# The out projection's last four columns by token tile, and a later place for tile 1's half

## The chip, the cores and the metric

The kernel runs on one core of a Trainium2 chip. The metric is the device time of one execution in microseconds (us). Three runs of the kernel before took 1156.49, 1156.77 and 1157.5 us; the median is 1156.77 us. The engines are TensorE (PE; its weight loads are PEld), VectorE (DVE), ScalarE (ACT), GpSimd (POOL) and SyncE (SP, which only issues DMAs).

## The reference, cut to what matters

There are 256 tokens of width 1024, everything is float32. A first block is run once, then two layers of a second block. Of the first block, this is what the change touches:

```
x = x + gate1 * (y_mix @ w_out)                              # out projection, 1024 x 1024
h2 = rms_norm(x, norm2_w) * (1.0 + scale2) + shift2
q = (h2 @ peer_wq).reshape(..., 8 heads, 2, 128)             # queries of eight expert heads
s = einsum('bqhpd,hpnd->bqhpn', q, peer_subkeys)             # scores of 2 x 128 keys
vals, idx = top_k(s, 16); combo = all 256 sums; top_s, pos = top_k(combo, 16)
u_sel = peer_u[expert]; a = gelu(einsum('bqhkd,bqd->bqhk', u_sel, h2))
x = x + gate2 * einsum('bqhk,bqhkd->bqd', softmax(top_s) * a, peer_v[expert])
```

`gate1`, `scale2`, `shift2` and `gate2` come from a modulation, `silu(c) @ w_ada + b_ada`. Each of 256 tokens picks 16 of 16384 experts for each of 8 heads, and for each pick a row of `peer_u` and one of `peer_v` is fetched: 2048 floats, 8 KB.

## The kernel before, in words

The 256 tokens are two tiles of 128. Activations lie feature by token: `xT[:, c, :]` holds features 128c to 128c+127 of all tokens, c = 0 to 7. Each engine runs its own program in the order in which it is written, and engines wait for one another's counters (semaphores), so that the order in which lines stand in an engine's program sets the order of the work.

**Out projection.** Each weight piece (128 output columns) is split by ScalarE and VectorE into two rounded parts (`split_hi`, L699, and `split_lo`, L706), and the activations too. A product is then three TensorE matmuls for each of eight 128-feature chunks (`by_parts`, L1447 to L1449): 24 matmuls of 256 tokens for a column of 128 features. Columns 0 to 3 are written to two PSUM banks (`held_out`), and columns 4 to 7 follow by `whole(mixed_in, 2)`, twice. After each column VectorE adds it to `xT` (L2210, the last one by tile, L2221), and ScalarE squares the sum (L1184) and multiplies it by the norm's gain (`gain_x`, L1174, for tile 0; L1179 for tile 1). TensorE adds the squares over features with a matrix of ones (`out_sums`, L1674); it does so in three places between the columns.

**First head.** Head 0's query for tile 0 is computed before the norm's root is known: `query_products` (L1689) on `xg`, then `early_scores_of_head_0` (L1767, L1768); the root's reciprocal is multiplied on the scores afterwards (`scores_of_head_0`, L2015). `route_first` then picks the first 8 of head 0's 16 experts for tile 0, `route_rest` the others. The normed `hT` of both tiles (`second_norm`, L2001) is shifted (L1211), turned to token-major (`turn_h2`, L1702), and used for the other queries (`score_query`, L1717) and keys (L1730).

**Gathers.** There are 16 groups (2 tiles x 8 heads) of 16 picks. Pick n is one indirect DMA of GpSimd (L997) of 128 rows of 8 KB, 1 MB, into one of 14 places. The places are six pairs in `rows`, seven in `low_pairs` (where the rounded parts and the squares of the projection lie before) and one slot of the weight ring; `FIRST_ROUND` gives their order. GpSimd waits before a place's first use until what lay there has been used, and later until `pair_used` says that TensorE has added the pick before. VectorE multiplies a gathered row by the token (`dot`, L2293), ScalarE sums it (L1260), takes gelu (L1271) and scales a diagonal (L1276), and TensorE adds the weighted second half of the row to the sum in PSUM (L1742). VectorE also chooses the experts of group g + 2 while group g is worked on (`route_halves`, `route_pairs`, `route_experts`); the second group's choice, `route(1)`, stands behind the first group's dots 0 to 3 and two more (`DOTS_AHEAD = 2`).

**Other work around it.** The modulation's 48 tiles are multiplied and summed on VectorE (`ada_dots`, L1965; the last two, `last_ada_tile`, L1975), those for `scale2` to `gate2` between the columns of the out projection. SP loads the expert heads' weights, and at the end of the out projection (`proj` at `M1`) the first weight unit of the second block's layers into `low_pairs[:, 1, :]` (L873). Where TensorE waits for ScalarE's copy of head 0's scores, it runs eight matmuls whose result nobody reads (L1803).

```
            whole(mixed_in, 2)
            out_sums(0, 1, 2, 3)
            whole(mixed_in, 2)
            out_sums(4, 5)
```

Of the kernel before, what the change touches and what calls it, by code (L numbers as in the profile page):

```python
# [14 lines left out]
ALU = mybir.AluOpType  # L15
# [32 lines left out]
PLACES = [("rows", 0), ("rows", 1), ("low", 2), ("low", 3), ("low", 4), ("low", 5), ("rows", 2), ("rows", 3), ("rows", 4), ("rows", 5),  # L48
          ("low", 0), ("low", 6), ("ring", 0), ("low", 7)]
LAST_ROUND = tuple(range(10))  # L50
# [3 lines left out]
AHEAD = 2  # L54
DOTS_AHEAD = 2
EXPERTS = 4
# [249 lines left out]
def first_of(*place):  # L306

    return PLACE_OF.index(PLACES.index(place))
# [55 lines left out]
def build(nc, a, out):  # L364
    ctx = ExitStack()
    with ctx:
# [53 lines left out]
        class Area:  # L420
# [66 lines left out]
        FIRST_HEADS_AT = ADA_RING * D  # L487
        own_place = {OWN_UNIT: own_unit, HELD_QUERY: low_pairs[:, 7, :], LAST_QUERY: extra[:, 0:2 * D], N1: low_pairs[:, 1, :]} | {n: extra[:, 2 * D + 512 * i:2 * D + 512 * i + 512] for i, n in enumerate(SUB_UNITS)} | \
            {n: flat[:, FIRST_HEADS_AT + 2 * D * i:FIRST_HEADS_AT + 2 * D * i + AT_1[n + 1] - AT_1[n]] for i, n in enumerate(FIRST_HEADS)}
# [137 lines left out]
        def chunk_out(m, width=T):  # L627
            b, j, _, _ = SEATS_1[m]
            z = aux[:, 3 + b, :] if b < BATCH else pj[:, b % 2, :]
            return z[:, j * T:j * T + width]  # L630

        conv_sums = chunk_out(M1 - KC + 2)

        def chunk_wait(eng, m):
# [149 lines left out]
        def tile_of(t):  # L784
            return slice(t * P, (t + 1) * P)
# [39 lines left out]
        def _(sp):  # L825
# [21 lines left out]
            for n in LOAD_ORDER:  # L847
# [75 lines left out]
        def _(pool):  # L923
# [45 lines left out]
            for g in range(NT * EXPERT_HEADS):  # L969
# [6 lines left out]
                for j in range(PICKS):  # L976
# [41 lines left out]
        def _(act):  # L1018
# [162 lines left out]

            for c in range(KC - 1):
# [4 lines left out]
                if c < KC - 2:  # L1187
                    gain_x(c)
                if c in (1, 3):
                    round_to(31 if c == 1 else 32)  # L1190
                if c in (3, 4, 5):
                    gain_x_of_tile_1(2 * c - 6, 2 * c - 5)
            act.wait_ge(taken_dve, KC)
            nc.scalar.activation(sq[:, KC - 1, 0:P], xT[:, KC - 1, 0:P], ACT.Square).then_inc(squares, 1)
            gain_x(KC - 2)
            gain_x(KC - 1)
            act.wait_ge(taken_dve, KC + 1)
            nc.scalar.activation(sq[:, KC - 1, P:T], xT[:, KC - 1, P:T], ACT.Square).then_inc(squares, 1)
            gain_x_of_tile_1(KC - 2, KC - 1).then_inc(xg_ready, 1)

# [230 lines left out]
        def _(pe):  # L1431
# [236 lines left out]

            def out_sums(*columns, tiles=range(NT)):

                for k in columns:
                    for t in tiles:
                        pe.wait_ge(squares, k + 1 if k < KC - 1 else KC + t)
                        ins = mm(aux[:, 2 + t, 0:P], ones[:, :], sq[:, k, t * P:(t + 1) * P], start=(k == 0), stop=(k == KC - 1))  # L1674
                        if k == KC - 1:
                            ins.then_inc(sums, 1)
# [127 lines left out]
            pe.wait_ge(taken_dve, KC + 1)  # L1804
            pe.wait_ge(h_ready, 2 * KC)
# [149 lines left out]
        def _(dve):  # L1955
# [247 lines left out]

            for c in range(KC):
                if c in (2, 4):
                    low_to(28 + c)
                m = M1 - KC + c
                chunk_wait(dve, m)
                if c < KC - 1:
                    v.scalar_tensor_tensor(xT[:, c, :], chunk_out(m), mod[:, 2 * KC + c:2 * KC + c + 1], xT[:, c, :], ALU.mult, ALU.add) \  # L2210
                        .then_inc(taken_dve, 1)
                    if c in (2, 3):
                        ada_dots(38 + c, 39 + c)
                    elif c in (4, 5):
                        ada_dots(34 + 2 * c, 36 + 2 * c)
                    if c == 5:
                        last_ada_tile(0)
                else:
                    for t in range(NT):
                        ts = slice(t * P, (t + 1) * P)  # L2220
                        v.scalar_tensor_tensor(xT[:, c, ts], chunk_out(m)[:, ts], mod[:, 2 * KC + c:2 * KC + c + 1], xT[:, c, ts], ALU.mult, ALU.add) \  # L2221
                            .then_inc(taken_dve, 1)
            last_ada_tile(1)
            last_ada_bias()
            dve.wait_ge(taken_dve, KC + 1)
            rstd_by_token()
            second_rstd(0)
            second_norm(0)
            scores_of_head_0()
# [144 lines left out]

            route_first()
            second_rstd(1)
# [331 lines left out]
```

## Time and profile before

| | |
|---|---|
| median of 3 runs | 1156.77 us |
| profiled execution, its own time | 1157.3 us |
| span of that execution's instructions | 1155.3 us |
| PE busy | 1040.5 us (90%) |
| DVE busy | 855.9 us (74%) |
| ACT busy | 708.2 us (61%) |
| POOL busy | 344.8 us (30%) |
| gathers (software queue q0) | 268.45 MB |
| weights and inputs (queue q1) | 120.10 MB |

The shares of busy time are means over stages with different limits: until about 165 us the first block's projections and attention, then the gathers, then the two layers of the second block. In the page's strip of 40 slices (28.9 us each) the DMA engines move 421 GB/s in nearly every slice from the 8th to the 28th.

### The profile page before, as it was taken

The numbers are of one execution on the slowest core, as the hardware profiler recorded it, in microseconds if no ns is written. First come the engines' busy times: TensorE is split into PE (matmuls) and PEld (weight loads), VectorE is DVE, ScalarE is ACT, GpSimd is POOL, SyncE is SP. The second block draws the span as 40 slices with busy tenths as digits, with TensorE's granted clock in tenths as the row PEclk, the third lists the DMA queues.
The fourth block names the chain that finished last, engine by engine and source line by source line (L and its number), as shares of the span: only waits on it lengthen the run. The fifth ranks groups of instructions, "written<-read, shape, count | busy, mean of one in ns | idle before, by whom it ended". The sixth has DMA issues, their size and how long they took to land.

```text
span 1155.3 us, 13406 instructions
## 1 busy us (share of the span) xinstructions
PE 1040.5 (90%) x4687; PEld 724.8 (63%) x4687; DVE 855.9 (74%) x1525; ACT 708.2 (61%) x1410; POOL 344.8 (30%) x367
## 2 busy tenths in 40 slices
PE   8999998999999878778877877799999999999997
PEld 6999987554455333333333323299888888888885
DVE  6998987967677666766767776656677768886776
ACT  3635855777766776666677666761458554577451
POOL 1001014555544554545544544555000000400000
PEclk9999999999999999999988999999999999999999
DMA  9988869999999999999999999999954654455540
GB/s 371 407 332 305 342 233 410 421 421 421 421 421 422 421 421 421 421 418 420 422 398 423 422 421 421 422 415 420 358 217 163 238 186 178 178 187 186 206 155 37
DMA packets 59556, 390.00 MB, mean 338 GB/s; under 512 B 6881, under 2 KB 7905, under 8 KB 15714
## 3 DMA queue, kind: packets, MB, share of 16 engines
q0 software_dynamic: 36864, 268.45, 56.1%
q1 hardware_dynamic: 21152, 120.10, 27.7%
q8 instruction: 37, 0.61, 0.2%
q10 hardware_dynamic: 1474, 0.60, 0.2%
q14 instruction: 29, 0.24, 0.1%
HBM read 388.08 MB, written 1.05 MB: 337 GB/s over the span
## 4 chain that ended last, share of the span: by engine, by line
PE 53%; DMA 27%; ACT 7%; issue 6%; DVE 5%; POOL 1%; SPq 0%; ACTq 0%; POOLq 0%; DVEq 0%
PE aux L1742 15%; DMA rows<-in_peer_uv,work 12%; DMA low_pairs<-in_peer_uv,work 12%; PE pj L1795 6%; PE pj L1796 6%; PE pj L1797 6%; PE pj L1855 5%; PE aux L1717 3%; PE pj L1856 3%; PE aux L1748 3%; ACT low_pairs L1260 2%; DMA wring<-in_peer_uv,work 2%; ACT L1271 1%; PE pj L1447 1%; DMA rows<-in_w_ada 1%
## 5 line engine op out<-in xcount | busy, mean ns | idle before, releaser
L1742 PE MATMUL aux<-rows,work 128*128 128x512 f32 x480 | 230.0, 630 | 49.9 <-ACT work L1276 49.9
L1742 PE MATMUL aux<-low_pairs,work 128*128 128x512 f32 x384 | 184.3, 629 | 37.5 <-ACT work L1276 37.5
L1742 PEld LDWEIGHTS aux<-rows,work 128*128 128x128 f32 x480 | 94.5, 201 | 176.5 <-issue 109.2
L997 POOL DMA_INDIRECT rows<-in_peer_uv,work x140 | 135.5, 968 | 227.3 <-PE aux L1742 146.9
L1260 ACT ACTIVATE rows<-rows 128x1024 f32<-128x1024 f32 x128 | 134.6, 1052 | 80.0 <-DVE rows L2293 79.7
L1742 PEld LDWEIGHTS aux<-low_pairs,work 128*128 128x128 f32 x384 | 75.6, 201 | 138.8 <-issue 87.2
L1260 ACT ACTIVATE low_pairs<-low_pairs 128x1024 f32<-128x1024 f32 x104 | 109.3, 1051 | 62.5 <-DVE low_pairs L2293 62.4
L775 DVE TENSOR_TENSOR wlo<-wring,whi 128x1024 fp32r<-128x1024 f32 x98 | 121.1, 1251 | 32.5 <-ACT whi L769 31.7
L997 POOL DMA_INDIRECT low_pairs<-in_peer_uv,work x108 | 103.5, 958 | 125.3 <-PE aux L1742 107.2
L769 ACT CAST whi<-wring 128x1024 fp32r<-128x1024 f32 x98 | 101.4, 1050 | 51.3 <-PE pj L1856 26.6
L2293 DVE TENSOR_TENSOR rows<-rows,aux 128x1024 f32<-128x1024 f32 x66 | 80.0, 1219 | 53.2 <-DMA rows<-in_peer_uv,work 52.8
L2293 DVE TENSOR_TENSOR low_pairs<-low_pairs,pj 128x1024 f32<-128x1024 f32 x58 | 70.1, 1218 | 45.1 <-DMA low_pairs<-in_peer_uv,work 44.3
L2293 DVE TENSOR_TENSOR rows<-rows,pj 128x1024 f32<-128x1024 f32 x62 | 74.7, 1217 | 38.5 <-DMA rows<-in_peer_uv,work 38.3
L1855 PE MATMUL pj<-x_parts,whi 128*128 128x512 f32 x256 | 91.3, 400 | 0.1
L1276 ACT ACTIVATE work<-work 128x128 f32<-128x128 f32 x248 | 79.3, 390 | 8.9 <-POOL work L966 3.1
L2293 DVE TENSOR_TENSOR low_pairs<-low_pairs,aux 128x1024 f32<-128x1024 f32 x46 | 55.8, 1219 | 35.8 <-DMA low_pairs<-in_peer_uv,work 35.3
L1447 PE MATMUL pj<-x_parts,whi 128*128 128x256 f32 x256 | 73.5, 287 | 0.4 <-DVE wlo L706 0.2
L1795 PE MATMUL pj<-whi,x_parts 128*128 128x512 f32 x184 | 72.6, 395 | 0.0
L1448 PE MATMUL pj<-x_parts,whi 128*128 128x256 f32 x256 | 72.5, 283 | 0.0
L1449 PE MATMUL pj<-x_parts,wlo 128*128 128x256 f32 x256 | 72.5, 283 | 0.0
L1856 PE MATMUL pj<-x_parts,wlo 128*128 128x256 f32 x256 | 72.0, 281 | 0.0
L1797 PE MATMUL pj<-wlo,x_parts 128*128 128x512 f32 x184 | 71.8, 390 | 0.0
(351 smaller groups left out, 2067.6 us busy)
## 6 DMA issues: line engine op xcount, KB each, us to landing
wring<-in_w SPq DMA_DIRECT2D x74, 1024.0 KB, 4.9
rows<-in_w_ada SPq DMA_DIRECT2D x46, 512.0 KB, 9.4
rows<-in_w SPq DMA_DIRECT2D x3, 1024.0 KB, 11.5
rows<-in_peer_uv,work POOLq DMA_INDIRECT x140, 12.8
low_pairs<-in_w SPq DMA_DIRECT2D x2, 1024.0 KB, 7.5
work<-in_late_rows SPq DMA_DIRECT2D x2, 1024.0 KB, 9.2
xT<-in_gate_rows SPq DMA_DIRECT2D x2, 1024.0 KB, 6.8
rows<-in_norm_rows SPq DMA_DIRECT2D x2, 1024.0 KB, 7.2
```

The source lines that it names most:

```text
L769: nc.scalar.copy(layer_part("hi", l, p), layer_raw(l, p)).then_inc(w_hi, 1)
L775: dve.tensor_tensor(layer_part("lo", l, p), layer_raw(l, p), full(layer_part("hi", l, p)), ALU.subtract).then_inc(w_lo["d"], 1)
L997: pool.indirect_dma_start(out=pair(n), out_offset=None, in_=a["peer_uv"], in_offset=bass.IndirectOffsetOnAxis(ap=expert[g % EXPERTS][:, j: ...
L1260: nc.scalar.activation(pair(n)[:, 0:D], pair(n)[:, 0:D], ACT.Copy, accum_out=dots[g % 2][:, j:j + 1]).then_inc(dotted, 1)
L1276: nc.scalar.activation(diag[:, j, :], diag[:, j, :], ACT.Copy, scale=act_dots[g % 2][:, j:j + 1]).then_inc(diag_ready, 1)
L1447: mm(o, w[0], x[0], start=start, stop=False, skip_group_check=skip)
L1742: ins = mm(peer_sum[t][:, half(c)], diag[:, n % PICKS, :], pair(n)[:, D + c * 512:D + (c + 1) * 512], start=(n % (EXPERT_HEADS * PICKS) == ...
L1795: mm(bank(u), hi[:, k, ts], w_hi_[:, j, :], start=(k == 0), stop=False)
L1797: ins = mm(bank(u), hi[:, k, ts], w_lo_[:, j, :], start=False, stop=(k == last))
L1855: mm(both, w_hi_[:, k, :], x_parts[:, :, k, :], start=(k == 0), stop=False, skip_group_check=True)
L1856: ins = mm(bank(u)[:, 0:T], w_lo_[:, k, :], xh[:, k, :], start=False, stop=(k == KC - 1), skip_group_check=True)
L2293: v.tensor_tensor(row, row, h2_tok[g // EXPERT_HEADS], ALU.mult).then_inc(multiplied, 1)
```

## The change

Columns 4 to 7 of the out projection are no longer multiplied for all 256 tokens at once. `tile_products(0)` multiplies the four columns for tile 0's 128 tokens, and `tile_products(1)`, for tile 1, stands behind `early_scores_of_head_0`. Sums of squares are made once for each tile behind its columns (`out_sums(t)`). VectorE adds columns 0 to 3 whole, columns 4 to 7 of tile 0 next, and those of tile 1 behind `route_first`. The modulation's dots move: 42 to 44 behind tile 0's columns, 45 and the last two behind `route_rest`. ScalarE's squares and gains follow the new order. `DOTS_AHEAD` goes from 2 to 0, so that `route(1)` stands ahead of dot 4. The idle matmuls go from eight to four. The layers' first weight unit goes to `low_pairs[:, 0, :]` and waits for tile 1's second column; the gathers use `low_pairs[:, 1, :]` instead. GpSimd gets three new waits.

```
-          ("low", 0), ("low", 6), ("ring", 0), ("low", 7)]
+          ("low", 1), ("low", 6), ("ring", 0), ("low", 7)]
-DOTS_AHEAD = 2
+DOTS_AHEAD = 0
+KEEP_BUSY = 4
...
+        TILES_FROM = M1 - HC
+        def tile_out(c, t):
+            if c < KC - 1:
+                return chunk_out(TILES_FROM, 512)[:, (c - HC) * P:(c - HC + 1) * P]
+            return chunk_out(M1 - 2)[:, t * P:(t + 1) * P]
+        def tile_wait(eng, c, t):
+            eng.wait_ge(proj, TILES_FROM + t * HC + (HC - 1 if c < KC - 1 else HC))
+        def taken_of(c, t):
+            return c + 1 + (t * HC if c >= HC else 0)
...
-            sp.wait_ge(proj, M1)
+            sp.wait_ge(proj, M1 + 2)
             sp.dma_start(own_place[N1], a["w2"][0, 0]).then_inc(own_loaded[own_group(N1)], 16)
...
+                    if n == first_of("rows", 1):
+                        pool.wait_ge(ada_used, RING_TILES - 1)
+                    if n == first_of("low", 2):
+                        pool.wait_ge(proj, M1 + HC)
+                    if n == first_of("low", 6):
+                        pool.wait_ge(sums, 1 + NT)
...
+            def square_tile(c, t):
+                act.wait_ge(taken_dve, taken_of(c, t))
+                nc.scalar.activation(sq[:, c, halves_[t]], xT[:, c, halves_[t]], ACT.Square).then_inc(squares, 1)
...
-            root(0)
             for s in range(2):
                 act.wait_ge(early_products, s + 1)
                 nc.scalar.copy(pq[:, 0, s, 0:P + 1], aux[:, 4 + s, 0:P + 1]).then_inc(early_query_out, 1)
+            root(0)
             act.wait_ge(early_products, 3)
             nc.scalar.copy(s_all[:, 0, :], aux[:, 1, 0:2 * KEYS]).then_inc(early_query_out, 1)
+            for c in range(HC, KC - 1):
+                square_tile(c, 1)
+            gain_x_of_tile_1(*range(HC, KC - 1))
+            square_tile(KC - 1, 1)
+            gain_x_of_tile_1(KC - 1).then_inc(xg_ready, 1)
             root(1)
...
-            whole(mixed_in, 2)
-            out_sums(0, 1, 2, 3)
-            whole(mixed_in, 2)
-            out_sums(4, 5)
+            def tile_products(t):
+                ts = tile_of(t)
+                for c in range(HC, KC):
+                    n = first_tiled + c - HC
+                    split_wait(pe, n)
+                    hi, lo = parts(n)
...
+                    for k in range(KC):
+                        xh_, xl_ = mixed_in(k)
+                        ins = by_parts(tile_out(c, t), (hi[:, k, :], lo[:, k, :]), (xh_[:, ts], xl_[:, ts]), k == 0, k == KC - 1, skip=True)
+                    ins.then_inc(proj, 1)
+            def out_sums(t):
+                for k in range(KC):
+                    pe.wait_ge(squares, taken_of(k, t))
+                    ins = mm(aux[:, 2 + t, 0:P], ones[:, :], sq[:, k, t * P:(t + 1) * P], start=(k == 0), stop=(k == KC - 1))
+                ins.then_inc(sums, 1)
+            tile_products(0)
...
             for s in range(2):
-                query_products(s, range(HC))
-            out_sums(6, 7, tiles=(0, ))
+                query_products(s, range(KC - 1))
             for s in range(2):
-                query_products(s, range(HC, KC)).then_inc(early_products, 1)
-            out_sums(6, 7, tiles=(1, ))
+                query_products(s, (KC - 1, )).then_inc(early_products, 1)
+            out_sums(0)
...
             early_scores_of_head_0()
+            tile_products(1)
+            out_sums(1)
             pe.wait_ge(early_query_out, 3)
-            for _ in range(8):
+            for _ in range(KEEP_BUSY):
...
+            for c in range(HC):                                  # VectorE: columns 0 to 3 whole
...
+                if c == 1:
+                    low_to(30)
+            low_to(32)
+            ada_dots(40, 42)
+            for c in range(HC, KC):
+                add_tile(c, 0)
+            ada_dots(42, 45)
             rstd_by_token()
-            second_rstd(0)
-            second_norm(0)
             scores_of_head_0()
...
             route_first()
+            for c in range(HC, KC - 1):
+                add_tile(c, 1)
+            second_rstd(0)
+            add_tile(KC - 1, 1)
+            second_norm(0)
             second_rstd(1)
             second_norm(1)
             route_rest()
+            ada_dots(45, RING_TILES)
+            for n in range(LAST_TILES):
+                last_ada_tile(n)
+            last_ada_bias()
```

## Rows read from the trace of the kernel before

**Rows 1.** The page, part 3: queue, kind, packets, MB, share of 16 engines.
```profile
q0 software_dynamic: 36864, 268.45, 56.1%
```

**Rows 2.** Stretches: us, engines' busy time (instructions), PEclk, DMA share, GB/s.
```profile
165.00:170.00 5.00, 4.76 (x26) 3.90 (x25) 4.62 (x20) 2.96 (x10) 0.51 (x1) 1.00 0.00 0
220.00:400.00 180.00, 167.87 (x478) 88.11 (x477) 124.85 (x231) 128.89 (x278) 93.99 (x99) 0.98 1.01 421
...
600.00:800.00 200.00, 162.24 (x621) 94.30 (x620) 129.34 (x210) 125.25 (x267) 103.40 (x109) 0.93 1.01 419
```

**Rows 3.** Timeline of TensorE: start, us, engine, line, operation, out<-in, count.
```profile
145.49 0.28 PE L1447 MATMUL pj<-x_parts,whi 128*128 128x256 f32 x1
...
151.25 1.95 PE L1674 MATMUL aux<-low_pairs,ones 128*128 128x128 f32 x16
...
158.79 1.05 PE L1674 MATMUL aux<-low_pairs,ones 128*128 128x128 f32 x8
159.68 1.95 PE L1689 MATMUL aux<-work,rows 128*128 128x129 f32 x16
...
164.82 0.39 PE L1768 MATMUL aux<-rows,pq 128*128 128x128 f32 x2
```

**Rows 4.** Timeline of TensorE, narrow f32 products of the attention.
```profile
124.19 1.90 PE L1604 MATMUL aux<-work,rows 128*128 128x64 f32 x16
125.92 1.95 PE L1638 MATMUL pj<-low_pairs,ones 128*128 128x256 f32 x8
```

**Rows 5.** Timeline of TensorE's weight loads behind a stall.
```profile
134.10 0.19 PEld L1447 LDWEIGHTS pj<-x_parts,whi 128*128 128x128 f32 x1 [0.34 <-DVE x_parts L2175]
134.20 0.19 PEld L1448 LDWEIGHTS pj<-x_parts,whi 128*128 128x128 f32 x1
```

**Rows 6.** Timeline of GpSimd, issues of gathers 0, 1, 2, 12 and 21.
```profile
169.49 1.18 POOL L997 DMA_INDIRECT rows<-in_peer_uv,work  x1 [53.56 <-DVE work L2333]
170.97 1.21 POOL L997 DMA_INDIRECT rows<-in_peer_uv,work  x1 [0.30 <-issue]
172.48 0.93 POOL L997 DMA_INDIRECT low_pairs<-in_peer_uv,work  x1 [0.30 <-issue]
...
197.09 0.98 POOL L997 DMA_INDIRECT wring<-in_peer_uv,work  x1
...
220.09 0.94 POOL L997 DMA_INDIRECT rows<-in_peer_uv,work  x1 [3.73 <-PE aux L1742]
```

**Rows 7.** DMA issues, last number us to landing: gathers 0, 1, 12, 21.
```profile
rows<-in_peer_uv,work POOLq DMA_INDIRECT x1, 5.8
rows<-in_peer_uv,work POOLq DMA_INDIRECT x1, 9.0
wring<-in_peer_uv,work POOLq DMA_INDIRECT x1, 10.2
rows<-in_peer_uv,work POOLq DMA_INDIRECT x1, 9.6
```

**Rows 8.** Timeline of SP's queue: the layers' first weight unit.
```profile
158.98 0.33 SPq L873 DMA_DIRECT2D low_pairs<-in_w  x1
```

**Rows 9.** Timeline of VectorE and ScalarE: tile, root, reciprocal, multiply, dots 0 and 3.
```profile
160.62 1.22 DVE L1975 CUSTOM_DVE_ANT_0 work<-work,rows 128x1024 f32<-128x1024 f32 x1
162.12 0.36 ACT L1204 ACTIVATE rstd<-aux,eps 128x128 f32<-128x128 f32 x1
163.07 0.94 DVE L1995 RECIPROCAL rstd<-rstd 128x128 f32<-128x128 f32 x1
170.14 1.23 DVE L2001 TENSOR_TENSOR hT<-hT,rstd 128x1024 f32<-128x1024 f32 x1
176.55 1.22 DVE L2293 TENSOR_TENSOR rows<-rows,pj 128x1024 f32<-128x1024 f32 x1
184.97 1.22 DVE L2293 TENSOR_TENSOR low_pairs<-low_pairs,pj 128x1024 f32<-128x1024 f32 x1 [1.27 <-DMA low_pairs<-in_peer_uv,work]
```

**Rows 10.** The chain that ended last, in order of time, 140 to 210 us.
```profile
188.91 6.91 PE aux L1717 x32
```

More of the change, by code:

```diff
@@ L487, in build @@
         FIRST_HEADS_AT = ADA_RING * D
-        own_place = {OWN_UNIT: own_unit, HELD_QUERY: low_pairs[:, 7, :], LAST_QUERY: extra[:, 0:2 * D], N1: low_pairs[:, 1, :]} | {n: extra[:, 2 * D + 512 * i:2 * D + 512 * i + 512] for i, n in enumerate(SUB_UNITS)} | \
+        own_place = {OWN_UNIT: own_unit, HELD_QUERY: low_pairs[:, 7, :], LAST_QUERY: extra[:, 0:2 * D], N1: low_pairs[:, 0, :]} | {n: extra[:, 2 * D + 512 * i:2 * D + 512 * i + 512] for i, n in enumerate(SUB_UNITS)} | \
             {n: flat[:, FIRST_HEADS_AT + 2 * D * i:FIRST_HEADS_AT + 2 * D * i + AT_1[n + 1] - AT_1[n]] for i, n in enumerate(FIRST_HEADS)}
@@ L1180, in gain_x_of_tile_1 @@
                 return ins
-            for c in range(KC - 1):
+            def square_tile(c, t):
+                act.wait_ge(taken_dve, taken_of(c, t))
+                nc.scalar.activation(sq[:, c, halves_[t]], xT[:, c, halves_[t]], ACT.Square).then_inc(squares, 1)
+            round_to(30)
+            for c in range(HC):
                 act.wait_ge(taken_dve, c + 1)
@@ L1186, in _ @@
                     nc.scalar.copy(xg[:, :, P:P + 1], mod[:, 3 * KC:4 * KC].unsqueeze(2)).then_inc(xg_ready, 1)
[L1187 to L1195, printed above, removed]
+                gain_x(c)
+                if c < 2:
+                    round_to(31 + c)
+            gain_x_of_tile_1(*range(HC))
+            for c in range(HC, KC - 1):
+                act.wait_ge(taken_dve, taken_of(c, 0))
+                gain_x(c)
+            square_tile(HC, 0)
+            act.wait_ge(taken_dve, taken_of(KC - 1, 0))
             gain_x(KC - 1)
-            act.wait_ge(taken_dve, KC + 1)
-            nc.scalar.activation(sq[:, KC - 1, P:T], xT[:, KC - 1, P:T], ACT.Square).then_inc(squares, 1)
-            gain_x_of_tile_1(KC - 2, KC - 1).then_inc(xg_ready, 1)
+            for c in range(HC + 1, KC):
+                square_tile(c, 0)
             def root(t):
@@ L1667, in _ @@
                 ins.then_inc(proj, 1)
[L1669 to L1676, printed above, removed]
-            whole(mixed_in, 2)
-            out_sums(0, 1, 2, 3)
-            whole(mixed_in, 2)
-            out_sums(4, 5)
+            def tile_products(t):
[4 more added lines that the diff above has]
+                    hi, lo = parts(n)
+                    if t:
+                        pe.wait_ge(taken_dve, taken_of(KC - 2 if c < KC - 1 else KC - 1, 0))
+                    else:
+                        pe.wait_ge(taken_dve, 2 if c < KC - 1 else HC)
+                    for k in range(KC):
[7 more added lines that the diff above has]
+                ins.then_inc(sums, 1)
+            first_tiled = piece[0]
+            tile_products(0)
             query_of_head_0 = w_slot(FIRST_HEADS[0])
@@ L1800, in _ @@
             early_scores_of_head_0()
+            tile_products(1)
+            out_sums(1)
             pe.wait_ge(early_query_out, 3)
-            for _ in range(8):
+            for _ in range(KEEP_BUSY):
                 mm(aux[:, 1, 0:2 * P], ident[:, :], wsT[:, 0:2, :].rearrange("p g t -> p (g t)"), start=True, stop=True)
-            pe.wait_ge(taken_dve, KC + 1)
+            pe.wait_ge(taken_dve, KC + HC)
             pe.wait_ge(h_ready, 2 * KC)
@@ L2202, in _, with add_tile @@
             second_gain()
-            for c in range(KC):
-                if c in (2, 4):
-                    low_to(28 + c)
+            def add_tile(c, t):
+                ts = slice(t * P, (t + 1) * P)
+                tile_wait(dve, c, t)
+                v.scalar_tensor_tensor(xT[:, c, ts], tile_out(c, t), mod[:, 2 * KC + c:2 * KC + c + 1], xT[:, c, ts], ALU.mult, ALU.add) \
+                    .then_inc(taken_dve, 1)
+            for c in range(HC):
                 m = M1 - KC + c
                 chunk_wait(dve, m)
[L2209 to L2225, printed above, removed]
+                v.scalar_tensor_tensor(xT[:, c, :], chunk_out(m), mod[:, 2 * KC + c:2 * KC + c + 1], xT[:, c, :], ALU.mult, ALU.add) \
+                    .then_inc(taken_dve, 1)
+                if c == 1:
[5 more added lines that the diff above has]
+            ada_dots(42, 45)
             rstd_by_token()
-            second_rstd(0)
-            second_norm(0)
             scores_of_head_0()
@@ L2375, in _ @@
             route_first()
+            for c in range(HC, KC - 1):
+                add_tile(c, 1)
+            second_rstd(0)
+            add_tile(KC - 1, 1)
+            second_norm(0)
             second_rstd(1)
```

## The prediction

> **What bounds the kernel now.** I read the queues and the stretches first. The gathers of the expert rows are 268.45 MB, and from 220 us to 800 us the DMA engines are busy all the time at 419 to 421 GB/s [rows 1, 2], while no compute engine is full. One gather is 1.05 MB and so takes 2.49 us. So the middle of the program is a queue of 256 gathers, and two things set its end: when it starts, and whether it ever runs dry. Between 165 and 170 us nothing moves at all [rows 2]: this hole in front of the first gather is what an edit can shorten.
>
> Then the timelines of TensorE, VectorE and GpSimd around the hole. TensorE multiplies the out projection's last four columns from 145.49 to 158.79 (96 products of 256 columns, and 16 sums of squares between them), then makes head 0's query and keys until 165.04 [rows 3], VectorE chooses eight experts, and GpSimd issues the first gather at 169.49 [rows 6].
>
> Last, how far the queue is ahead of its consumers. The first gather, alone in the queue, landed 5.8 us after its issue. The 13th (index 12, issue 197.09) took 10.2 us and the 22nd (index 21, issue 220.09) 9.6 us [rows 6, 7], so they lay 4.4 and 3.8 us behind others. Those are the margins: an issue that comes later by more than that leaves the queue empty. Up to the 13th gather the chain of waits runs not through the queue but from the first group's dots over ScalarE to head 2's query on TensorE [rows 9, 10].
>
> **The change, step by step.** All sums are against the profiled execution, 1157.3 us, 0.5 us above the median of the runs (1156.77); I add the difference to the median.
>
> (1) Tile 0's half of the last four columns: 4 x 8 x 3 = 96 products of 128 moving columns instead of 256. Before shows no such product of rounded parts. A 256-column one starts every 0.12 us (48 from 145.49 to 151.25) [rows 3]. If only the columns counted, a 128-column one would take 0.06. But the products in plain f32 don't get cheaper with fewer columns: 16 records of 64 columns took 1.73 us, 0.108 each, and 8 of 128 columns 0.89, 0.111 each [rows 4, 3]; each loads its own weights. After a stall the second weight load of the rounded parts starts 0.10 us after the first [rows 5], long before a matmul's columns could hold it up. So I take 0.108, the weight load's pace: 10.4 us for tile 0, done at 155.9. Ends: 0.06 (columns alone) and 0.21 (two f32 records for each product, were narrow products run like plain f32).
>
> The Trainium skill ("TensorE: Matmul & The Clock Gate", section "Back-to-back issue gap") gives about 81 ns for a matmul of 128 columns in a stream of load and matmul. By it tile 0 would be done at 153.3. The 0.108 of the narrow f32 rows speaks against it; no row here shows it for rounded parts.
>
> (2) From there to the first gather: before 6.25 us (158.79 to 165.04: sums, query, scores). After: the query's 3.6, tile 0's 16 sum records in 1.7, scores 0.9, together 6.2. The choice of eight experts is unchanged. First gather: 2.9 + 0.1 = 3.0 us earlier, at 166.5.
>
> (3) The layers' first weight unit (1 MB, SP) was issued at 158.98 into the empty queue [rows 8]. It now waits for tile 1's second column: 162.0 + 48 x 0.108 = 167.2, behind the first gather. It takes 2.49 us of a queue that is full from there: the lead shrinks to 0.5 us.
>
> (4) Tile 1's 96 products and 16 sums now stand behind the first head's keys: 162.0 + 10.4 = 172.4. VectorE idles from the end of the first choice (166) until tile 1's three columns are there (170). Then come the last column's add, square and sum (0.3 us each, estimated from the root's 0.36), root, reciprocal (0.94) and the multiply for tile 1 (1.1) [rows 9]: done at 176.9, where before the multiply began at 170.14 and the choice's rest ended at 176.55. The rest takes 5.3 us, to 182.2.
>
> (5) Three dots of the modulation (1.15 each) and the bias, before beside the projection, now stand between that and the first dot: 3.8 us, 186.0. The first four dots (4.7 us) end at 190.8. Before, they waited for data, and the fourth began at 184.97: it comes 4.7 us later.
>
> (6) From the fourth dot the chain is as before: ScalarE's sum, head 1's keys, head 2's query (6.9 us on TensorE [rows 10]), its keys, the first weighted sums, whose ends free the places for the 14th gather on. So the 13th and 14th gathers issue 4.7 us later, the later ones some 5.0, as dots 5 and 6 now stand behind the second group's choice and that behind head 2's scores; score_query(3) on TensorE hides nearly all of it.
>
> (7) Sum at the queue: index 12 is late by 4.7 - 4.4 = 0.3 us, index 21 by 5.0 - 3.8 = 1.2. The largest counts: +1.2. The lead of (3) lies before it and is lost. Starting from nearly empty costs more: behind the first gather the second landed not 2.49 but 4.7 us later (issue 170.97 plus 9.0 against 169.49 plus 5.8 [rows 6, 7]), a loss of 2.2. Here it is between nothing and that; I take 1.1. Together **+2.3 us: 1159.1**.
>
> At nothing: the third gather waits for tile 1's products (172.6, before 172.48 [rows 6]) with the first two and the weight unit in the queue until 176. The ninth waits for the last modulation dots (185.9), which has cover: it lands seven gathers behind the second, which landed at 180.0, so at 197.4, and an issue at 191.6 would still do. Half of the keep-busy products go, at a place where TensorE waits anyway. The low places that change sides, the earlier splits of the last two pieces and ScalarE's new order have idle time around them. If (5)'s dots had other cover, 3.8 us would come back, more than the margin lacks.
>
> **Rivals.**
> A. Columns set the pace, wholly (0.06 us) or half way to the weight load (0.084). For it: no narrow product of rounded parts is in the trace. Against: the f32 rows. The first gather comes 7.6 to 5.2 us earlier; the weight unit, issued 1.4 us before it or right with it, takes 0.7 to 2.5 of that; the consumers are 4.5 us early to 0.4 late, within the margins. 1149.9 to 1154.1, say 1152. The skill's 81 ns would be a case of A, 1153.7; of A's chance I give it a third.
> B. Narrow products cost two f32 records, 0.21 us. For it: f32 128 x 128 is recorded so; against: the rounded 256-column rows show no second record. Tile 1 ends 20 us later, so index 21 is late by 25 - 3.8, and with the restart: 1179.
> C. Not slower: the pace is as in (1), but the consumers' delay stays under the margin. It decides at the fourth dot: if it comes less than 3.5 us later (begins before 188.5), the queue never empties and the start alone counts: 0.5 us, or up to 2.5 if the weight unit only fills the 2.2 us that the start loses anyway. 1154.3 to 1156.3, say 1155.5. For it: VectorE has 4 us idle at 166 to 170, and each hop of (4) is estimated; against: (4) and (5) are in strict order on VectorE.
>
> **How the numbers follow.** Forecast 49%; its own range, from pace 0.106 and no restart loss to 0.12 and the whole loss, is +0.8 to +5.7: 1157.6 to 1162.5. A 18%, B 10%, C 23%. A measurement of this kernel tells 0.2%, 2.3 us, from no change; the forecast sits on that bound: of its 49, 25 slower, 22 same, 2 faster. A: 16 faster, 2 same. B: slower. C: 12 faster, 11 same. Faster 30%, same 35%, slower 35%. The range holds the forecast, C and about half of A: 1151.0 to 1163.5; B and A's far end stay outside.
>
> **What would show it.** Right: narrow products start every 0.11 us; the first gather near 166.5; the weight unit's load between the first two gathers; the fourth dot near 189.6; between 195 and 230 us stretches of the DMA under 400 GB/s. Wrong in (1): starts every 0.06 to 0.08 us, first gather before 164. Wrong in (4) or (5): fourth dot before 188.5 and the DMA at 420 GB/s throughout; then the end moves by the start alone. B: starts every 0.2 us, first gather after 175.

## The result and the profile after

The changed kernel is slower: 1162.8 us (median of 6 runs, 1161.25 to 1164.03) against 1157.11 us for the kernel before beside it (6 runs), a ratio of 1.0049, 95% interval 1.0037 to 1.0061, so 4.3 to 7.1 us. The two profiled executions lie 4.0 us apart (1161.25 and 1157.3; spans 1159.3 and 1155.3).

The start went as forecast. TensorE's timeline of the changed kernel: the narrow products start every 0.11 us (145.83, 145.94, 146.05), and tile 0 is done at 156.22, where the query begins.
```profile
145.83 0.27 PE L1479 MATMUL pj<-x_parts,whi 128*128 128x128 f32 x1
145.94 0.27 PE L1480 MATMUL pj<-x_parts,whi 128*128 128x128 f32 x1
146.05 0.28 PE L1481 MATMUL pj<-x_parts,wlo 128*128 128x128 f32 x1
...
156.22 3.79 PE L1733 MATMUL aux<-work,rows 128*128 128x129 f32 x32
```
GpSimd's issues of gathers 0, 12 and 21 (index from 0), and SP's load of the layers' first weight unit, again the changed kernel. Against [rows 6, 8] the first gather is 2.5 us earlier, index 12 is 5.4 us later, index 21 6.6 us later, and the unit now stands behind the first gather and ahead of the second.
```profile
166.97 1.18 POOL L1019 DMA_INDIRECT rows<-in_peer_uv,work  x1 [51.00 <-DVE work L2373]
...
202.50 1.26 POOL L1019 DMA_INDIRECT wring<-in_peer_uv,work  x1
...
226.66 0.94 POOL L1019 DMA_INDIRECT rows<-in_peer_uv,work  x1 [3.73 <-PE aux L1785]
```
```profile
168.03 0.33 SPq L889 DMA_DIRECT2D low_pairs<-in_w  x1
```
What that did to the queue is read from three stretches (columns as in [rows 2]; the last number is GB/s). The kernel before:
```profile
165.00:180.00 15.00, 12.40 (x69) 11.20 (x69) 12.03 (x47) 8.09 (x25) 8.07 (x9) 0.89 0.55 199
180.00:200.00 20.00, 17.27 (x81) 13.74 (x80) 14.66 (x42) 11.25 (x24) 7.73 (x9) 1.00 1.01 424
200.00:230.00 30.00, 30.00 (x94) 16.74 (x93) 27.65 (x61) 23.42 (x49) 16.24 (x18) 1.00 1.01 421
```
The changed kernel, the same stretches:
```profile
165.00:180.00 15.00, 13.85 (x117) 13.32 (x117) 8.96 (x29) 7.07 (x25) 7.22 (x7) 1.00 0.74 294
180.00:200.00 20.00, 17.12 (x97) 15.11 (x96) 16.06 (x49) 11.45 (x26) 6.15 (x7) 1.00 1.02 424
200.00:230.00 30.00, 28.59 (x91) 16.29 (x90) 29.49 (x57) 21.39 (x45) 13.91 (x14) 1.00 0.90 339
```
TensorE's granted clock is 1.00 in all three rows of the changed kernel, so the clock is not what lost the time here. The rows make a ledger. Stretch times GB/s gives the bytes moved; from them I take the weight unit (1.05 MB) where it is loaded inside, and divide what is missing against before by 421 GB/s. By 200 us the changed kernel has moved 12.89 MB, 11.84 of them gathers, against 11.47: 0.9 us ahead. Between 200 and 230 us it moves 10.17 MB instead of 12.63: 5.8 us lost. By 230 us it is 2.09 MB, 5.0 us, behind. From there to 580 us both go at 421 GB/s, so this is most of the difference. In five-microsecond pieces all six from 200 to 230 us lie below 421, this one lowest (the others 328 to 413):
```profile
200.00:205.00 5.00, 4.49 (x20) 2.85 (x19) 4.83 (x18) 2.45 (x4) 2.45 (x3) 1.00 0.55 184
```
The gather of index 12 landed 5.8 us after its issue (the view of DMA issues), as long as the first one alone in the queue took in [rows 7]: the queue was dry when it came.
```profile
wring<-in_peer_uv,work POOLq DMA_INDIRECT x1, 5.8
```
Who was late is in VectorE's timeline of the changed kernel: idle until tile 1's columns (170.71), the three modulation dots from 183.08, the first dots at 186.90, the fourth half way through the next pair, at 190.4, and then 3.39 us of waiting for ScalarE's copy of head 1's scores before the second group's choice.
```profile
170.71 0.87 DVE L2253 SCALAR_TENSOR_TENSOR xT<-pj,mod,xT 128x128 f32<-128x128 f32 x3 [4.04 <-PE pj L1481]
...
183.08 1.22 DVE L2010 CUSTOM_DVE_ANT_0 rows<-rows 128x1024 f32<-128x1024 f32 x1
...
186.90 2.35 DVE L2333 TENSOR_TENSOR rows<-rows,pj 128x1024 f32<-128x1024 f32 x2
...
189.24 2.33 DVE L2333 TENSOR_TENSOR low_pairs<-low_pairs,pj 128x1024 f32<-128x1024 f32 x2
194.97 0.49 DVE L2282 MAX8 work<-work 128x8 f32<-128x128 f32 x2 [3.39 <-ACT work L1253]
```
There is one later difference. Near 600 us the kernel before falls below the full rate itself (the two rows below), and the changed kernel less (422 and 389 GB/s in the same two pieces). By 780 us the ledger has gone from 5.0 to 3.9 us.
```profile
596.00:600.00 4.00, 4.00 (x11) 1.83 (x10) 3.81 (x10) 2.09 (x6) 2.64 (x4) 1.00 0.94 340
600.00:604.00 4.00, 4.00 (x10) 1.71 (x9) 2.99 (x5) 3.68 (x7) 2.25 (x3) 1.00 1.01 352
```

### The profile page after: what moved, and what is told of

Read it like the earlier page. It is cut to its first block, busy times and chain, and to the rows that moved or that the text cites. A ratio compares the mean times of both kernels' runs of the same rounds, so it can differ in the third digit from the quotient of the medians.

```text
span 1159.3 us, 13594 instructions
## 1 busy us (share of the span) xinstructions
PE 1050.4 (91%) x4775; PEld 730.4 (63%) x4775; DVE 857.6 (74%) x1528; ACT 708.7 (61%) x1413; POOL 344.2 (30%) x367
## 3 DMA queue, kind: packets, MB, share of 16 engines
HBM read 388.08 MB, written 1.05 MB: 336 GB/s over the span
## 4 chain that ended last, share of the span: by engine, by line
PE 53%; DMA 27%; ACT 10%; DVE 8%; issue 2%; SPq 1%; POOL 0%; ACTq 0%; DVEq 0%; POOLq 0%
PE aux L1785 15%; DMA rows<-in_peer_uv,work 12%; DMA low_pairs<-in_peer_uv,work 10%; PE pj L1838 6%; PE pj L1839 5%; PE pj L1840 5%; PE pj L1900 5%; PE pj L1901 3%; DMA rows<-in_w_ada 3%; PE pj L1479 2%; ACT low_pairs L1292 2%; PE pj L1480 2%; PE pj L1481 2%; PE aux L1760 2%; DMA wring<-in_peer_uv,work 2%
## 5 line engine op out<-in xcount | busy, mean ns | idle before, releaser
L1785 PE MATMUL aux<-rows,work 128*128 128x512 f32 x480 | 232.4, 635 | 42.8 <-ACT work L1308 42.8
L1785 PE MATMUL aux<-low_pairs,work 128*128 128x512 f32 x384 | 188.3, 641 | 38.4 <-ACT work L1308 38.4
L1479 PE MATMUL pj<-x_parts,whi 128*128 128x256 f32 (+1 forms) x288 | 81.9, 284 | 0.4 <-DVE wlo L722 0.3
L1480 PE MATMUL pj<-x_parts,whi 128*128 128x256 f32 (+1 forms) x288 | 80.9, 281 | 0.0
L1481 PE MATMUL pj<-x_parts,wlo 128*128 128x256 f32 (+1 forms) x288 | 80.9, 281 | 0.0
L1901 PE MATMUL pj<-x_parts,wlo 128*128 128x256 f32 x256 | 71.8, 281 | 0.0
```

Of the source, the lines that this page charges most:

```text
L1479: mm(o, w[0], x[0], start=start, stop=False, skip_group_check=skip)
L1480: mm(o, w[0], x[1], start=False, stop=False, skip_group_check=skip)
L1481: return mm(o, w[1], x[0], start=False, stop=stop, skip_group_check=skip)
L1785: ins = mm(peer_sum[t][:, half(c)], diag[:, n % PICKS, :], pair(n)[:, D + c * 512:D + (c + 1) * 512], start=(n % (EXPERT_HEADS * PICKS) == ...
L1901: ins = mm(bank(u)[:, 0:T], w_lo_[:, k, :], xh[:, k, :], start=False, stop=(k == KC - 1), skip_group_check=True)
```

## The experiments

Theory E: the queue is dry at gathers 12 to 21 because VectorE's dots come late, and the end follows that. Rivals: the weight unit in front of the gathers is the cost (U); in the runs of moved dots, the first gathers' pace is what counts (G). All times stand beside runs of the kernel before on the same chip (1156.9 to 1157.3 us).

**1. e1_two_dots_ahead.** The fifth and sixth dot back ahead of the second group's choice.
```diff
-DOTS_AHEAD = 0
+DOTS_AHEAD = 2
```

> The changed kernel with DOTS_AHEAD back to 2. Theory, an empty queue: in the changed kernel the second group's choice waits 3.4 us for head 1's scores (start 194.97) while dots 4 and 5 stand behind it. With the two dots ahead they fill that wait; dot 7 ends 2.3 us earlier, the fifth weighted sum on TensorE begins 0.9 us earlier (it then waits for head 3's first query half), and the gathers from the 18th on come 0.9 us earlier. Gathers 12 and 13 are untouched. Time 0.9 us under the changed kernel's (about 1161.9). Rival, the weight unit or the extra TensorE work is the cost: no difference. Rival, the order of dots is the main cost: 3 us or more under it.

1161.33 us, ratio 1.0032 (1.0020 to 1.0045), which overlaps the changed kernel's interval. The trace shows what the number alone doesn't: the dots did close the distance between index 12 and 21, from 24.16 us to 23.00, as in [rows 6], but index 12 itself was 1.65 us later. TensorE's granted clock was 0.57 in the mean from 193 to 197 us, so mostly at the lower of its two levels (1.2 GHz), just as it took up head 1's keys after 2.44 us of idling; the changed kernel idles there as long and has 1.00. So this profiled execution is 0.08 us off the changed kernel's, and the run decides little. Five of its six runs took 1161.28 to 1161.42 us and one 1159.16; whether that one kept the higher clock, no trace shows. Gathers 12 and 21, and the stretch:
```profile
204.15 0.99 POOL L1019 DMA_INDIRECT wring<-in_peer_uv,work  x1
...
227.15 0.95 POOL L1019 DMA_INDIRECT rows<-in_peer_uv,work  x1 [3.72 <-PE aux L1785]
```
```profile
193.00:197.00 4.00, 3.68 (x14) 3.39 (x15) 1.95 (x8) 1.75 (x3) 0.95 (x1) 0.57 1.01 420
```

**2. e2_mod_dots_in_idle.** The last three modulation dots and the bias go into VectorE's idle time before tile 1.
```diff
             route_first()
+            ada_dots(45, RING_TILES)
+            for n in range(LAST_TILES):
+                last_ada_tile(n)
+            last_ada_bias()
...
             route_rest()
-            ada_dots(45, RING_TILES)
-            for n in range(LAST_TILES):
-                last_ada_tile(n)
-            last_ada_bias()
```

> The changed kernel with the last three modulation dots and their bias moved into VectorE's idle time behind the first choice (166.6 to 170.7 us). Theory, an empty queue: the first dot starts 3.8 us earlier (183.1), but head 1's query on TensorE then ends last (190.8), so head 1's keys and all behind come 2.0 us earlier: gather 12 at 200.5, which leaves the queue just not empty; a hole of about 1.3 us stays at gathers 17 and 18. Time 3 to 4.4 us under the changed kernel's: 1158.4 to 1159.8. Rival, the weight unit in the queue or TensorE's extra 10 us: no difference (1162.8).

1158.98 us, 1.0017 (1.0008 to 1.0026): by the medians 3.8 us come back. That the moved work takes as much on VectorE (183.08 to 186.90 above) is in part chance. The dots begin 3.5 us earlier (183.42), but head 1's query on TensorE now ends last (191.1), so that the second group's choice, index 12 (200.96) and index 21 (225.11) come only 1.5 us earlier, and the ledger gains 1.6.
```profile
193.43 0.49 DVE L2282 MAX8 work<-work 128x8 f32<-128x128 f32 x2 [5.34 <-ACT work L1253]
```
From 200 to 230 us the queue moves 367 GB/s in place of 339: E holds. Unexpected: the first two gathers took longer to issue (last section).

**3. e3_both_moves.** Both edits.

> Both edits of the two runs before together. Theory, an empty queue: gathers 12 and 13 2.0 us earlier, 17 and 18 2.9 us earlier than in the changed kernel; almost no hole is left and the start's lead of 0.9 us counts: 1156.2 to 1157.5, no slower than before the change. Rivals: weight unit or TensorE's work, 1162.8; dots' order alone, as with DOTS_AHEAD 2 alone.

1157.61 us, 1.0007 (0.9997 to 1.0016): no longer told from before, 0.1 us above the range expected. By the medians the two moves together give back 5.2 of 5.7 us, with the weight unit and TensorE's extra work still in: those are not what cost the time. Beside e2 the two dots are worth 1.4 us: the choice begins when it did there (193.36, in e2 193.43), and from index 12 (200.88) to 21 (223.88) it is 23.00 us again. In e1 the wait ahead of the choice had room for the dots too (2.05 us of it were left); there the lower clock took the gain.

**4. e4_two_loads.** The narrow products cheaper: the weights' high part is loaded once for 256 moving columns (both parts of the tile's input), the low part for 128; VectorE adds the two halves.
```diff
-  ins = by_parts(tile_out(c, t), (hi[:, k, :], lo[:, k, :]), (xh_[:, ts], xl_[:, ts]), k == 0, k == KC - 1, skip=True)
+  mm(tile_out(c, t), hi[:, k, :], x_parts[:, :, k, ts], start=(k == 0), stop=False, skip_group_check=True)
+  ins = mm(tile_out(c, t)[:, 0, :], lo[:, k, :], xh_[:, ts], start=False, stop=(k == KC - 1), skip_group_check=True)
```

> The changed kernel with the tile products made from two weight loads a chunk instead of three: the high weights once, over 256 moving columns (the tile's high and low activations side by side), and the low weights once over 128; VectorE adds the two halves with one more operation each. Theory, the weight load sets the pace (0.111 us for a narrow product): a column takes 8 x (0.12 + 0.111) = 1.85 us instead of 2.67, a tile 7.4 instead of 10.7; the first gather comes 3 us earlier (164.0), tile 1 ends 6.6 us earlier, no hole is left in the queue, and the start counts: 3 to 4 us under the kernel before (1153 to 1154). Rival, the columns set the pace (0.06 us for 128): a column would take 8 x 0.18 = 1.44. Rival, one third fewer instructions saves nothing because the adds on VectorE are what the chain waits for: first gather 1 us or less earlier.

1157.13 us, 1.0000 (0.9991 to 1.0009): a miss. The products do start every 0.23 us for two, where three took 0.33, and the first gather goes out at 164.01, 5.5 us before [rows 6]. But index 12 is issued at 197.31 and the consumers are no earlier than in before: TensorE takes up head 1's keys at 188.00, in before at 187.78.
```profile
145.81 0.34 PE L1712 MATMUL pj<-x_parts,whi 128*128 128x256 f32 x1
145.99 0.23 PE L1713 MATMUL pj<-x_parts,wlo 128*128 128x128 f32 x1
146.05 0.33 PE L1712 MATMUL pj<-x_parts,whi 128*128 128x256 f32 x1
```
```profile
164.01 1.18 POOL L1017 DMA_INDIRECT rows<-in_peer_uv,work  x1 [47.97 <-DVE work L2380]
...
197.31 1.26 POOL L1017 DMA_INDIRECT wring<-in_peer_uv,work  x1
```
The stretches of this run show the lead made and lost: 389 GB/s in place of 199 up to 180, then 392 and 381 in place of 424 and 421. Its ledger at 230 us is 0.1 us behind before.
```profile
165.00:180.00 15.00, 12.81 (x93) 11.59 (x93) 12.06 (x35) 9.40 (x30) 8.29 (x8) 1.00 0.99 389
180.00:200.00 20.00, 17.06 (x80) 13.59 (x79) 16.12 (x53) 11.22 (x23) 7.86 (x9) 1.00 0.97 392
200.00:230.00 30.00, 29.11 (x90) 16.20 (x89) 27.52 (x55) 22.32 (x48) 15.45 (x17) 1.00 0.98 381
```
The slack of [rows 7] is not a constant: a queue that starts x us earlier and goes at the same rate meets each late gather x us sooner. A lead and a margin are the same microseconds.

**5. e5_unit_later.** The changed kernel, the weight unit loaded where the queue is full.
```diff
             sp.wait_ge(proj, M1 + 2)
+            sp.wait_ge(queries, 10)
```

> The changed kernel with one more wait: the layers' first weight unit (1 MB) is loaded only after head 5's first query product, near 262 us, where the queue of gathers is full, instead of at 168.0, ahead of the third gather. Theory E (the queue runs dry at gathers 12 to 21 because VectorE's dots come late): the unit lies today in time that the queue loses anyway, so taking it out there gains nothing and putting it in later costs its 2.49 us: 1165.3 (1164.5 to 1166.5), gathers 12 to 21 issued as in the changed kernel. Theory U (the unit in front of the gathers is what costs): the same bytes elsewhere, 1160.3 to 1162.8.

1164.65 us, 1.0056 (1.0042 to 1.0069). By the medians alone, 1.85 us above the changed kernel with overlapping intervals, U is unlikely and not excluded. The stretches settle it: with a megabyte less to carry, the gathers were issued as before the edit (index 12 at 202.63, 21 at 226.77) and moved no more: 22.04 MB by 230 us, where the changed kernel's gathers had 22.01. The unit had filled time that was empty anyway.
```profile
165.00:180.00 15.00, 13.85 (x117) 13.32 (x117) 8.96 (x30) 6.95 (x24) 7.14 (x7) 1.00 0.68 250
180.00:200.00 20.00, 17.11 (x97) 15.13 (x96) 16.06 (x49) 11.57 (x26) 6.23 (x8) 1.00 1.01 421
200.00:230.00 30.00, 28.61 (x92) 16.40 (x91) 29.48 (x57) 21.28 (x45) 13.92 (x14) 1.00 0.87 329
```

**6. e6_mod_dots_in_wait.** The modulation dots at another place: behind the first group's four dots, in the wait for head 1's scores.
```diff
             for j in range(GROUP, GROUP + DOTS_AHEAD):
                 dot(0, j)
+            ada_dots(45, RING_TILES)
+            for n in range(LAST_TILES):
+                last_ada_tile(n)
+            last_ada_bias()
             for g in range(1, AHEAD):
                 route(g)
```

> The changed kernel with the last three modulation dots and the bias moved behind the first group's four dots, where VectorE waits 3.4 us for head 1's scores. The first dot starts 3.8 us earlier, at 183.1, as in the run with the same dots behind the first choice, but here GpSimd's first gather is issued undisturbed (1.18 us, not 1.89) and the first data comes near 168.9. Theory E: the end is set by the holes at gathers 12 to 17, whose issue follows the dots (index 12 near 201.0, 17 near 214.8): 1159.0 (1158.2 to 1159.6), no better than that run. Theory G (the late first data cost that run its 3.3 us): 1155.5 to 1157.

1159.5 us, 1.0021 (1.0012 to 1.0030), not told from e2 and in the range of E, but with the hole at another place. Index 12 is at 200.83 (in e2 200.96), and from 200 to 230 us the queue moves 409 GB/s (in e2 367). It is dry earlier, at 224 GB/s from 190 to 195 us: the ninth gather (index 8) takes the place of the last modulation tiles, waits for the moved dots and goes out at 192.18, later than the 191.6 up to which the prediction gave it cover.
```profile
192.18 0.94 POOL L1019 DMA_INDIRECT rows<-in_peer_uv,work  x1 [10.77 <-DVE mod L2020]
```
```profile
180.00:200.00 20.00, 18.55 (x103) 16.07 (x101) 17.68 (x55) 11.97 (x28) 6.80 (x9) 1.00 0.93 372
```
So the equal time by itself does not rule out G. The bytes do: by 180 us e6 has moved 4.33 MB and e2 4.25, so the undisturbed first gathers (1.18 us for the first) were worth 0.2 us.

**7. e7_two_loads_dots_in_wait.** The edits of e4 and e6 together: the early start, and consumers that keep up with it.

> The two-weight-load products of the earlier run (first gather at 164.0) with the last three modulation dots and the bias behind the first group's four dots. Theory E: first dot at 177.9 in place of 181.7; head 1's query on TensorE (7.07 us from 178.5) is then what head 1's scores wait for, so the chain is 1.5 to 1.7 us early: index 12 issued near 195.7, index 17 near 209.5, 1155.4 (1154.6 to 1156.2), faster than the kernel before by 0.1 to 0.2 per cent. If the gathers' late issue is not what gave the lead back in that run, it stays at 1157.1.

1153.72 us, 0.9970 (0.9959 to 0.9981): faster than before, by more than I expected. The dots start 4.0 us before e4's (181.72), the choice 2.0 and index 12 2.1 us (197.31 in e4). The ninth gather waits for the modulation dots as in e6 (186.58), and the queue falls to 310 GB/s from 185 to 190 us.
```profile
177.69 2.35 DVE L2340 TENSOR_TENSOR rows<-rows,pj 128x1024 f32<-128x1024 f32 x2
...
187.78 0.49 DVE L2289 MAX8 work<-work 128x8 f32<-128x128 f32 x2 [1.70 <-ACT work L1251]
```
```profile
195.23 1.26 POOL L1017 DMA_INDIRECT wring<-in_peer_uv,work  x1
...
219.39 0.94 POOL L1017 DMA_INDIRECT rows<-in_peer_uv,work  x1 [3.73 <-PE aux L1784]
```

**8. e8_two_loads_wait_two_ahead.** e7 with `DOTS_AHEAD = 2`; the modulation dots then stand behind six dots, not four.

> As the run before this one, with the fifth and sixth dot again ahead of the second group's choice. Theory E: the dots fill what is left of VectorE's wait (1.7 us) and push the choice by 0.6, index 12 near 196.3, but index 17 on come 1.15 earlier relative to it, near 208.9; the last hole counts: 1154.9 (1154 to 1156). If the two dots ahead cost more than they give, 1156 to 1157.

1156.55 us, 0.9994 (0.9985 to 1.0003): a miss, by a wait that the prediction put at nothing and that I did not count again here, though e6 and e7 have it: the ninth gather waits for the modulation dots, here until 190.35. The queue went dry there instead, at 185 to 195 us.
```profile
190.35 0.94 POOL L1017 DMA_INDIRECT rows<-in_peer_uv,work  x1 [14.11 <-DVE mod L2019]
```
```profile
185.00:190.00 5.00, 4.45 (x25) 3.74 (x24) 4.86 (x9) 2.45 (x4) 0.00 (x0) 1.00 0.67 277
190.00:195.00 5.00, 4.38 (x21) 3.52 (x19) 4.83 (x25) 0.87 (x3) 4.07 (x5) 1.00 0.61 197
```

**9. e9_dots_ahead_behind_mod.** e8 with the modulation dots ahead of the fifth and sixth dot.

> As the run of two weight loads with two dots ahead (1156.55), but the three modulation dots and the bias stand before the fifth and sixth dot, not behind them. In that run the ninth gather waited for them until 190.35 and the queue ran dry there (it landed at 195.4, 6 us behind the eighth), while from the ninth on it never did again. Theory E: ninth gather issued near 186.5 again, index 12 near 196.3, index 21 near 218.4 (219.39 in the run without dots ahead, 1153.72): 1152.7 (1151.8 to 1153.8). If the two dots ahead cost by themselves and not through the ninth gather, it stays at 1156 to 1157.

1153.51 us, 0.9969 (0.9957 to 0.9981). The ninth gather is back at 186.76, and 3.0 us of e8 come back. Against e7 nothing can be told, though index 21 is 1.0 us earlier (218.41) and the ledger 1.3 us better; what took that back stays open (by 780 us the two ledgers below are 0.1 us apart).

**10. e10_one_mod_dot_early.** e9 with one modulation dot in the 1.57 us gap before tile 1's last two columns.
```diff
             second_rstd(0)
+            ada_dots(45, RING_TILES)
             add_tiles(1, 6, 7)
...
-            ada_dots(45, RING_TILES)
             for n in range(LAST_TILES):
                 last_ada_tile(n)
```

> As the run before this one, with one of the three modulation dots in VectorE's gap before tile 1's last two columns (1.57 us idle). Theory E: ninth gather near 185.4, the second group's choice 1.1 us earlier, index 12 near 195.3, index 21 near 217.3: 1151.4 (1150.4 to 1152.6). Against it: such a dot beside GpSimd's gather made that gather's issue longer (1.18 to 1.89 us in an earlier run), which could take the early start back: 1152.7.

1152.67 us, 0.9961 (0.9947 to 0.9974): the fastest version, 4.3 us below before and 10.1 below the changed kernel by the medians, though not told from e7 and e9. It lies just above the range expected: the ninth gather (185.55) and index 12 (195.35) came as forecast, index 21 at 218.35, 1.0 us late. The time is the one named against E (1152.7), but not by that mechanism: the first two gathers were issued in 1.18 and 0.94 us. From 200 to 230 us it runs at the full rate:
```profile
165.00:180.00 15.00, 12.81 (x94) 11.65 (x94) 13.34 (x36) 9.64 (x31) 8.17 (x8) 1.00 0.99 403
180.00:200.00 20.00, 18.94 (x85) 14.43 (x84) 19.09 (x60) 12.94 (x27) 9.03 (x10) 1.00 0.98 387
200.00:230.00 30.00, 30.00 (x94) 16.74 (x93) 25.57 (x50) 23.29 (x51) 16.69 (x19) 1.00 1.01 422
```

**11. e11_before_no_dots_ahead.** The kernel before with `DOTS_AHEAD = 0` alone.

> The kernel before with the one number changed: no dot ahead of the second group's choice. Theory E: index 17 on is issued some 1.15 us later, within the 3.8 to 4.4 us by which these gathers lie behind others: the queue doesn't run dry, no change, 1157.1 (1156.5 to 1158). If the late dots cost by themselves wherever the queue stands: 1158.2 to 1158.5.

1157.2 us, 1.0001 (0.9992 to 1.0010): no change. The distance from index 12 to 21 grows from 23.00 us [rows 6] to 24.15 and the queue doesn't notice (421 GB/s from 200 to 230). The edit that costs 1.4 us on a dry queue costs nothing on one with slack.
```profile
196.60 1.26 POOL L997 DMA_INDIRECT wring<-in_peer_uv,work  x1
...
220.75 0.95 POOL L997 DMA_INDIRECT rows<-in_peer_uv,work  x1 [3.72 <-PE aux L1742]
```

The ledger at 230 us, the same carried on to 780 us in stretches of 25 us, the profiled execution from which both are summed, and the medians, each against before, in us (plus is later):
```
            after  e1    e2    e3    e4    e5*   e6    e7    e8    e9    e10   e11
ledger 230  +5.0  +5.4  +3.4  +1.7  +0.1  +7.4  +2.6  -1.4  +0.2  -2.7  -3.1   0.0
ledger 780  +3.9  +4.2  +2.1  +1.6  -1.0  +7.2  +2.0  -3.3  -0.3  -3.4  -3.5  +0.6
profiled    +4.0  +4.0  +2.0  +0.2  -1.7  +7.4  +1.5  -3.6  -0.9  -3.7  -4.0  -0.1
median      +5.7  +4.4  +2.0  +0.7  +0.2  +7.3  +2.2  -3.6  -0.8  -3.5  -4.3  +0.2
* 4.9 at 230 us, and 2.5 for the unit that is still to come
```
At 230 us the ledger lies within 2.2 us of the execution that it was taken from, at 780 us within 0.7 (e3: 1.4). Part of what comes between is the stretch from 580 to 605 us, where before and e11 fall to 397 and 393 GB/s and no other run below 405. What is left is not explained here.

## Why the prediction was right, and where it was short

Slower was right, and the mechanism was the predicted one: a full queue that runs dry because the consumers come later. The size was short: +2.3 was forecast, +5.7 (4.3 to 7.1) came, inside the whole range but above the forecast's own 1157.6 to 1162.5.

- **(1) Right.** 0.111 us for a narrow product against 0.108: 156.2, forecast 155.9. Rivals A and B fell with it. It was not the columns that set the pace: 384 of them take 0.33 us as three products with a load each, and 0.23 in e4 as two. That fits the weight load, though no run parts a load from its product. The Trainium skill's 81 ns ("TensorE: Matmul & The Clock Gate", "Back-to-back issue gap") is not what this trace shows for rounded parts that load 128 fresh columns each. The Trainium skill's section "LDWEIGHTS (loading the stationary operand)" of the same page gives columns / 1.2 ns, by which an estimate for 128 is 107 ns; the 0.111 agrees with that.
- **(2), (3) Right.** First gather 166.97 (166.5), unit at 168.03 (167.2) behind it, lead 0.9 us (0.5).
- **(4), (5) Right in each hop, 0.8 us late in the sum.** Tile 1's products ended near 173.2, 0.8 us later than I had it (172.4), and nothing made that up: multiply done at 177.9 (176.9), first dot 186.90 (186.0), fourth 190.4 (189.6). So 5.4 us later than in [rows 9], not 4.7. That the moved dots would bring 3.8 us back if they had other cover came out in the medians (e2 3.8, e6 3.3), but partly by luck: index 12 came only 1.5 and 1.7 us earlier, because head 1's query on TensorE then ends last.
- **(6) Failed in its last clause.** Index 12 did follow the fourth dot (both +5.4). But "score_query(3) on TensorE hides nearly all of it" was wrong for dots 5 and 6: the distance from index 12 to 21 grew by 1.16 us, and e11 shows the same 1.15 with nothing else changed. Index 21 came 6.6 us later, not 5.0. The dots stand behind the second group's choice, which waits for head 1's scores (3.39 us), not for head 2's, as the prediction has it. TensorE, which in before went from score_query(3) to the next weighted sums without a gap, waits 0.90 us for ScalarE's diagonals now:
```profile
214.08 1.12 PE L1785 MATMUL aux<-low_pairs,work 128*128 128x512 f32 x2 [0.90 <-ACT work L1308]
```
- **(7) Two terms mis-sized.** By its own rule, 6.6 - 3.8 = 2.8 us of delay beyond the margin, where I had 1.2. And the restart: I took 1.1 of 0 to 2.2, for one emptying. The ledger's 5.0 leaves 5.0 - 2.8 = 2.2, the whole of it. That is not a measured restart but what is left; the rate stayed below 421 GB/s in all six pieces from 200 to 230 us, not once but at a series of gathers. So the forecast's +2.3 is short by 1.6 (delay) and 1.1 (restart).
- **At nothing: right for this kernel, by a limit that the later runs met.** The ninth gather went out at 187.37, with 421 and 426 GB/s from 185 to 195 us. In e6 it went out later than the 191.6 of the prediction, and the queue was dry.
- **What the ledger leaves.** Medians 5.7, ledger 5.0, profiled pair 4.0. The changed kernel's profiled execution is the shortest of its six; and the kernel before loses more near 600 us, so that the ledger is at 3.9 by 780 us. The restart above, taken as what is left of 5.0, is no surer than that.
- **Rival C** said that it decides at a fourth dot 3.5 us later. It came 5.4 later, and the other case held. C assumed that an early start counts in full while the consumers stay in the margin; e4 shows that it would not have: of 5.5 us of earlier first gather the weight unit took 2.5, and the other 3.0 were gone by 230 us (ledger +0.1), because the consumers stayed where they were.

## What to carry to other kernels

Where a long queue bounds the time, an earlier start is worth only what the consumers that free its places gain too: the margin of a late transfer shrinks by every microsecond that the queue starts earlier. Before moving work behind a first request, list what it now stands in front of, and put it into a wait that the trace shows (moving the three dots away from the first dot gave back 3.3 to 3.8 us in the medians). List also what waits for the work that you move: in e6 and e8 it was the ninth gather, and the hole moved there. And sum bytes by stretch: what was missing by 230 us told the end of a 1160 us program within some 2 us, and what was missing by 780 us within 0.7 in all runs but one.

## What the runs showed of the hardware

GpSimd's issue of a gather depends on what VectorE is doing when it begins. In e2 the first two took 1.89 and 1.75 us beside multiply-sums whose two inputs both lie in SBUF (the tiles `work` and `rows`), where the changed kernel has 1.18 and 0.93 with VectorE idle.
```profile
167.31 1.89 POOL L1019 DMA_INDIRECT rows<-in_peer_uv,work  x1 [51.01 <-DVE work L2373]
168.07 1.22 DVE L2020 CUSTOM_DVE_ANT_0 work<-work,rows 128x1024 f32<-128x1024 f32 x1
169.22 1.22 DVE L2020 CUSTOM_DVE_ANT_0 work<-work,rows 128x1024 f32<-128x1024 f32 x1
169.51 1.75 POOL L1019 DMA_INDIRECT rows<-in_peer_uv,work  x1 [0.30 <-issue]
```
In e4 the fourth gather took 1.67 us beside the multiply of `work` and `rstd` and the third 0.94 beside additions that read one of their large inputs from the products' tile `pj`. The order counts: the changed kernel's third gather began 0.10 us before such a multiply and took 0.94 us beside it.
```profile
173.63 0.94 POOL L1019 DMA_INDIRECT low_pairs<-in_peer_uv,work  x1 [4.24 <-PE pj L1481]
173.73 1.22 DVE L2046 TENSOR_TENSOR hT<-work,rstd 128x1024 f32<-128x1024 f32 x1
```
